# Other queue orders for the delta stage of a two-layer block on one Trainium2 core

## Chip, cores and metric

The kernel runs on one core of one Trainium2 chip. The metric is the device time of one execution in microseconds (us), lower is better. Times of several executions are given as their median.

## What is computed

Two transformer blocks, one after the other, over 256 positions of width 1024: the first has a gated feed-forward, an mLSTM mixer and a second feed-forward; the second has a gated delta rule layer, a feed-forward with a short convolution, a sliding-window attention and a last feed-forward. All in float32. Only the gated delta rule layer matters for this change:

```python
def gated_deltanet(hn, w_in, conv_w, a_log, dt_bias, out_norm_w, w_out):
    proj = hn @ w_in
    qkv, z, b, a = jnp.split(proj, [...], axis=-1)
    qkv = jax.nn.silu(causal_dwconv(qkv, conv_w))          # four taps
    q, k = l2norm(q) * 128 ** -0.5, l2norm(k)              # 8 heads, repeated to 16
    beta = jax.nn.sigmoid(b)
    g = -jnp.exp(a_log) * jax.nn.softplus(a + dt_bias)
    o = chunked_gated_delta_rule(q, k, v, g, beta)         # triangular solve, then hops
    o = rmsnorm_2(o, out_norm_w) * jax.nn.silu(z)          # 16 heads of 128
    return o.reshape(bsz, t, GDN_V_DIM) @ w_out
```

The solve inverts, for each head and chunk, a unit lower triangular matrix made of the products of the keys with a decay.

## The kernel before

Everything is a sequence of matrix products with weights streamed from HBM. A **unit** is 8 weight tiles of 128 x 128 (512 KB). For each unit SyncE (SP) loads it into one of four `raw` slots, ScalarE (ACT) makes its high part (`hi(j)`, `split_hi`, line 408), VectorE (DVE) or GpSimd (POOL) its low part (`lo(j)`, `split_lo`, line 417), and TensorE (PE) multiplies each tile three times (high x high, high x low, low x high) with 256 columns. A load waits for the low part of the unit four before it, a high part for PE's end of the unit four before it.

The delta stage is the class `GCore` (lines 1933 to 3314). It runs 52 units (`self.units`, numbered from 4 on PE), cut into **quarters** of two tiles, six matmuls: `d(h0, h1)` (line 3008) runs quarters h0 to h1 - 1, and quarter h is of unit h // 4. Between them stand the small products of the layer. The result banks rotate: `self.banks` gives the bank of unit j, `evicted` says which step empties it. The steps, by name:

- `sc`, `tap3_j`, `taps(j)`: scale, and the four taps of the convolution of unit j's result (ACT does tap 3, DVE taps 2 to 0). `zc`, `zx`, `zs`: the same for the gate z. `gzs(u)` scales the group u of z that was computed before the stage.
- `ggd1`, `ggd2`, `ggb` on DVE, `ea`, `gabs`, `exp_`, `ln_g`, `eb`, `gcs` on ACT: the decay g (its cumulative sum) and beta; `ggb` is an addition and the reciprocal of beta. `colsT` on PE transposes both and waits for both.
- `xs`, `xh`, `xl`: the normalised input in high and low part, for the units from 12 on. `qs`, `sq`, `ss`, `ln2`, `ln3`, `ex`, `kn`: Silu and L2 norm of q and k.
- `gk`, `mt`: products of keys, masked; `gather(g)`, `wld`: their diagonal blocks, through HBM, to one block per partition; `b(j)`: 31 steps of forward substitution on DVE in tile `gX`; `xt` (ACT): its transpose.
- `xd`, `xtd` (SP): stores of both to `x_d` and `xt_d`; `scatU` (4 DMAs, waits for `uzero`, a memset of POOL, which waits for `at(3)`) and `scatT` (3 DMAs) scatter the blocks back from there. Both wait for both stores. `gq`, `at`, `qd`: products of q and k, masked, and q with its decay.
- `c1` to `c8`, for four groups of heads: the rest of the solve, from 32-wide to 128-wide blocks, alternating PE (odd) with DVE (`c2`, `c6`) and ACT (`c4`, `c8`). `c1(0)` waits for all scatters.
- `p1` to `p7`, `e1` to `e6`, `kd`: the two chunks of the recurrence by group. `sqr`, `p7`, `rl`, `re`, `yz`, `yo`, `yh`, `yl`: norm, gate, and the high and low part of the result, which units 44 to 55 (`gout0`, `gout1`) multiply; unit 44 + 2u waits for `yl(u)`.

The order of each engine's queue is written out by hand in the methods `act`, `dve`, `pool`, `sync` and `pe`; the lists of names in `__init__` must repeat it, since a wait on a step is a wait on one counter per engine that has reached the place of that step in the list. Each engine executes its queue strictly in order, so a step that waits holds all behind it. `exp_and_log` (line 343) loads the ACT table that has Exp and Ln; where a Silu follows, another load comes by itself.

Of the kernel before, what the change touches and what calls it, by code (L numbers as in the profile page):

```python
# [154 lines left out]
def program(nc, a):  # L155
    with ExitStack() as ctx:
# [1637 lines left out]
        class GGateSteps:  # L1794
# [3 lines left out]
            def __init__(self, norm):  # L1798
                self.norm = norm
                self.dv = steps("dve", "ggate", ["a", "b", "pos", "b1", "beta", "gc0", "gc1"])  # L1800
                self.ac = steps("act", "ggate", ["abs", "eb", "exp", "ea", "ne", "ln", "gcs"])
# [131 lines left out]
        class GCore:  # L1933
# [5 lines left out]
            def __init__(self, gate, norm):  # L1939
                self.gate, self.norm = gate, norm  # L1940
                self.A = steps("act", "gdn_act", (
# [7 lines left out]
                    " yh3").split())  # L1949
                self.V = steps("dve", "gdn_dve", (  # L1950
# [13 lines left out]
                    " tap43_0 yl0 e1_3 e4_2 kd3 yz1 yo1 e1b_3 yz2 yl1 e4_3 yo2 yz3 yl2 yo3 yl3").split())  # L1964
                self.T = steps("pe", "gdn_pe", (
# [3 lines left out]
                    " p1k_3 p7_1 p5_2 p2_3 p6_2 p3_3 p1b_3 p7_2 p3b_3 p4_3 p5_3 p6_3 p7_3").split())  # L1969
                self.G = steps("pool", "gdn_pool", (  # L1970
                    "xzero col em0 em2 em3 xinit em1 br uzero tzero nb").split())
# [53 lines left out]
            def act(self, eng):  # L2025
# [186 lines left out]
                tap3(2)  # L2212
                tap3(0)
                tap3(1)
                hi(6)
                hi(7)
                exp_and_log(eng)
                tap3(3)
                gabs()
                eb()  # L2220
                exp_()
                ea()
                hi(8)
                tap3(4)
                ln_g()
                qs(0)
                gcs()
                tap3(5)
                hi(9)
                cols()  # L2230
                rp()
                tap3(6)
                hi(10)
                tap3(7)
                hi(11)
# [172 lines left out]
            def dve(self, eng):  # L2408
# [251 lines left out]
                for j in range(0, 4):  # L2660
                    b(j)
# [1531 lines left out]
```

How the kernel before makes its waits and increments, by code:

```python
    def wait(self, eng, it, name, back=0):  # L110
        n = len(self.names)
        eng.wait_ge(self.sem, (it + (1 - back)) * n + self.names.index(name) + 1)
# [216 lines left out]
        def unit_done(eng, st, it, u):  # L329
            eng.wait_ge(s_pe[u % SLOTS], turn(st, it, u) + 2)
# [7 lines left out]
        def evacuated(eng, st, it, g):  # L339
            eng.wait_ge(s_ev, group(st, it, g) + 5)
# [9 lines left out]
        def load_opening(eng, st, u):  # L351
            s = u % SLOTS
            eng.wait_ge(s_lo[s], turn(st, 0, u) + 1)
            eng.dma_start(raw[s][:, :, :].rearrange("p (g k) m -> p g k m", g=4),
                          st.weights[0].rearrange("p (g k) m -> p g k m", g=4)[:, :, 2 * u:2 * u + 2, :]
                          ).then_inc(s_raw[s], 16)
# [1 line left out]
        def load_keys(eng, u):  # L359
            eng.wait_ge(s_lo[u], turn(gqk0, 0, u) + 1)
            for b, s_body in enumerate((s_raw, s_kq)):
                eng.dma_start(raw[u][:, :, :].rearrange("p (g k) m -> p g (k m)", g=4)[:, 2 * b:2 * b + 2],
                              gqk0.weights[b].rearrange("p (g k) m -> p g (k m)", g=4)[:, 0:4:2, 2 * u * P:2 * (u + 1) * P]
                              ).then_inc(s_body[u], 16)
# [1 line left out]
        def load_pairs(eng, st, u):  # L367
            s = u % SLOTS
            eng.wait_ge(s_lo[s], turn(st, 0, u) + 1)
            eng.dma_start(raw[s][:, :, :].rearrange("p (g k) m -> p g (k m)", g=2),
                          st.weights[u % 2].rearrange("p (g k) m -> p g (k m)", g=2)[:, :, 4 * (u // 2) * P:
```

## Time and profile before

| | us |
|---|---|
| median of 3 runs | 1268.59 |
| lowest and highest | 1266.85, 1273.55 |
| profiled execution, its own time | 1265.16 |
| its span, first to last instruction | 1263.3 |
| PE / PE weight loads busy | 1238.2 (98%) / 1212.2 (96%) |
| DVE busy | 886.0 (70%) |
| ACT busy | 760.0 (60%) |
| POOL busy | 287.0 (23%) |
| mean granted TensorE clock | 0.995 |

The profiled execution is one run, 3.4 us under the median of the three. The delta stage runs from about 560 to 771 us of the span. PE's busy time is that of overlapping matmuls with modelled ends, so short stops don't show in it; the starts of the matmuls in the timeline do. Names of tiles in the rows are the program's: `gX`, `gXT` the substitution and its transpose, `gU`, `gT` the blocks, `dQK` q and k, `dVT` v, `wh`, `wl` the parts of the weights, `dZ` the gate, `H` the residual, `ACC` a sum of squares.

### The profile page before, as it was taken

Reading aid. Unit: us, or ns where it says so; the run is one execution under the profiler, and the core shown is the slowest. Engines: PE = TensorE matmul, PEld = TensorE weight load, DVE = VectorE, ACT = ScalarE, POOL = GpSimd, SP = SyncE. Lnnn points to the kernel's source line nnn. Section 1 sums busy time; section 2 is a strip of 40 time slices with the busy share of each in tenths; the row PEclk is TensorE's granted clock in tenths of the full one; section 3 lists DMA queues with packets and bytes.
Section 4 is the critical chain, followed back from the end, with each engine's and each line's share of the span. In section 5 each row is a group of like instructions: output and inputs, shape, how many; then the busy total and the mean of one; then the engine's idle time right before and its main releaser. Section 6 shows DMA issues by size and latency. Waiting matters only on the chain.

```text
span 1263.3 us, 28600 instructions
## 1 busy us (share of the span) xinstructions
PE 1238.2 (98%) x10498; PEld 1212.2 (96%) x10498; DVE 886.0 (70%) x1619; ACT 760.0 (60%) x1276; POOL 287.0 (23%) x243
## 2 busy tenths in 40 slices
PE   7999999999999999999999999999999999999997
PEld 7999999998999999999998989999999989999997
DVE  5866656887787665596777556777766797877654
ACT  6544444598555444469755686666665576766642
POOL 0000000010000000028875223344530131444400
PEclk9999999999999999999999999999999999999998
DMA  7655466464356656745646224855587525666473
GB/s 234 208 173 170 138 175 184 139 198 132 103 175 204 184 155 182 217 131 207 201 157 175 84 68 148 228 189 184 170 199 205 176 68 167 184 185 185 137 204 104
DMA packets 87804, 212.53 MB, mean 168 GB/s; under 512 B 19429, under 2 KB 34085, under 8 KB 87600
## 3 DMA queue, kind: packets, MB, share of 16 engines
q1 hardware_dynamic: 85536, 204.60, 53.7%
q0 software_dynamic: 1632, 6.46, 2.1%
q8 instruction: 49, 0.80, 0.3%
q10 hardware_dynamic: 560, 0.44, 0.1%
q14 instruction: 27, 0.22, 0.0%
HBM read 208.41 MB, written 3.06 MB: 167 GB/s over the span
## 4 chain that ended last, share of the span: by engine, by line
PE 89%; DVE 5%; ACT 3%; issue 2%; DMA 0%; POOL 0%; DVEq 0%; ACTq 0%; SPq 0%
PE bank L552 20%; PE bank L554 20%; PE bank L553 20%; PE bank L3002 3%; PE bank L3003 3%; PE bank L3004 3%; PE bank L525 1%; PE bank L1653 1%; PE bank L526 1%; PE bank L529 1%; PE bank L3137 1%; PE bank L1655 1%; PE bank L1654 1%; DVE wl L420 1%; PE bank L3654 1%
## 5 line engine op out<-in xcount | busy, mean ns | idle before, releaser
L415 ACT ACTIVATE wh<-raw 128x1024 fp32r<-128x1024 f32 (+3 forms) x423 | 407.4, 970 | 338.1 <-PE bank L554 286.4
L420 DVE TENSOR_TENSOR wl<-raw,wh 128x1024 fp32r<-128x1024 f32 (+3 forms) x350 | 384.6, 1102 | 138.7 <-ACT wh L415 138.1
L552 PE MATMUL bank<-XH,wh 128*128 128x256 f32 (+1 forms) x1448 | 410.7, 284 | 1.3 <-DVE XL L992 1.2
L554 PE MATMUL bank<-XH,wl 128*128 128x256 f32 (+1 forms) x1448 | 410.2, 283 | 0.0
L553 PE MATMUL bank<-XL,wh 128*128 128x256 f32 (+1 forms) x1448 | 409.9, 283 | 0.0
L552 PEld LDWEIGHTS bank<-XH,wh 128*128 128x128 f32 x1448 | 273.4, 189 | 2.1 <-DVE XL L992 1.4
L554 PEld LDWEIGHTS bank<-XH,wl 128*128 128x128 f32 x1448 | 273.7, 189 | 0.0
L553 PEld LDWEIGHTS bank<-XL,wh 128*128 128x128 f32 x1448 | 272.2, 188 | 0.0
L420 POOL TENSOR_TENSOR wl<-raw,wh 128x1024 fp32r<-128x1024 f32 x73 | 175.9, 2420 | 285.6 <-ACT wh L415 285.5
L552 PE MATMUL bank<-AH,wh 128*128 128x256 f32 (+1 forms) x704 | 198.7, 282 | 0.0
L554 PE MATMUL bank<-AH,wl 128*128 128x256 f32 (+1 forms) x704 | 198.5, 282 | 0.0
L553 PE MATMUL bank<-AL,wh 128*128 128x256 f32 (+1 forms) x704 | 198.2, 281 | 0.0
L553 PEld LDWEIGHTS bank<-AL,wh 128*128 128x128 f32 x704 | 132.8, 189 | 0.0
L554 PEld LDWEIGHTS bank<-AH,wl 128*128 128x128 f32 x704 | 132.3, 188 | 0.0
L552 PEld LDWEIGHTS bank<-AH,wh 128*128 128x128 f32 x704 | 132.1, 188 | 0.2
L3002 PE MATMUL bank<-gXH,wh 128*128 128x256 f32 x256 | 76.1, 297 | 1.8 <-DVE dVT L2452 1.8
L3003 PE MATMUL bank<-gXL,wh 128*128 128x256 f32 x256 | 72.2, 282 | 0.0
L3004 PE MATMUL bank<-gXH,wl 128*128 128x256 f32 x256 | 72.1, 282 | 0.0
L864 DVE TENSOR_TENSOR tp<-bank,R 128x256 f32<-128x256 f32 x88 | 37.3, 424 | 40.7 <-PE bank L554 33.2
L828 POOL TENSOR_TENSOR AL<-pr,AH 128x256 f32 (+1 forms) x44 | 36.6, 831 | 99.0 <-ACT AH L821 98.9
L3002 PEld LDWEIGHTS bank<-gXH,wh 128*128 128x128 f32 x256 | 48.9, 191 | 3.7 <-issue 3.2
L876 ACT ACTIVATE bank<-tp,vec 128x256 f32<-128x256 f32 x88 | 48.8, 554 | 4.5 <-DVE tp L864 4.5
(396 smaller groups left out, 2253.8 us busy)
## 6 DMA issues: line engine op xcount, KB each, us to landing
raw<-in_w_up SPq DMA_DIRECT2D x175, 512.0 KB, 4.4
raw<-in_w_down SPq DMA_DIRECT2D x64, 384.0 KB, 3.4
raw<-in_w_down SPq DMA_DIRECT2D x64, 320.0 KB, 3.2
raw<-in_w_gvz SPq DMA_DIRECT2D x32, 512.0 KB, 4.4
raw<-in_w_gout SPq DMA_DIRECT2D x16, 512.0 KB, 4.6
raw<-in_w_gqk SPq DMA_DIRECT2D x12, 512.0 KB, 4.6
raw<-in_w_mv SPq DMA_DIRECT2D x8, 512.0 KB, 4.6
raw<-in_w_mqk SPq DMA_DIRECT2D x8, 512.0 KB, 5.0
```

Source lines behind the costliest of these rows:

```text
L415: eng.activation(WH[s][:, 0:n, :], raw[s][:, 0:n, :], ACT.Copy).then_inc(s_hi[s], 1)
L420: eng.tensor_tensor(WL[s][:, 0:n, :], raw[s][:, 0:n, :], WH[s][:, 0:n, :].bitcast(F32), ALU.subtract).then_inc(s_lo[s], 1)
L525: eng.matmul(out, WH[u][:, 2 * g + j, :], xh, start=k == 0, stop=False)
L552: eng.matmul(out, WH[s][:, i, :], xh, start=start, stop=False)
L553: eng.matmul(out, WH[s][:, i, :], xl, start=False, stop=False)
L554: mm = eng.matmul(out, WL[s][:, i, :], xh, start=False, stop=stop)
L828: self.lows.done(eng.tensor_tensor(AL[:, bass.ds(j, 1), 0:T], PR[b][:, 0:T].unsqueeze(1), AH[:, bass.ds(j, 1), 0:T].bitcast(F32), ALU.subt ...
L864: leave(st, it, u, eng.tensor_tensor(TP[u % 2][:, 3:3 + T], bank[st.banks[u]][:, 0:T], R[:, 0:T], ALU.mult))
L876: self.tap2s.done(eng.activation(self.sums(u), TP[u % 2][:, 3:3 + T], ACT.Identity, bias=v(self.bias, m), scale=v(self.w, m + 88)), f"tap2 ...
L3002: eng.matmul(out, WH[s][:, i, :], xh, start=first, stop=False)
L3003: eng.matmul(out, WH[s][:, i, :], xl, start=False, stop=False)
L3004: mm = eng.matmul(out, WL[s][:, i, :], xh, start=False, stop=last)
```

## The change

The queues of the delta stage get another order on every engine, and the lists of names with them. No arithmetic is added or left out. One low part moves between engines in the sum: on DVE 13, 38, 43, 49, 50 become 14, 37, 50, 54; the others are POOL's. There are seven `exp_and_log` in both, at other places. The core of the diff:

```diff
 # pe: quarters between the small products
-                d(102, 104)
+                d(105, 107)
                 gq(0)
-                d(104, 115)
+                d(107, 113)
                 gq(1)
-                d(115, 132)
+                d(113, 128)
                 gq(2)
-                d(132, 136)
+                d(128, 133)
                 gq(3)
-                d(136, 156)
+                d(133, 148)
                 p1(0)
-                d(156, 158)
+                d(148, 159)
                 c1(0)
-                d(158, 159)
-                c1(1)
+                d(159, 161)
                 c3(0)
...
                 p6(3)
-                d(188, 191)
+                d(188, 190)
                 p7(3)
-                d(191, 208)
+                d(190, 208)
 # sync
                 xd()
                 xtd()
                 load(40)
-                load(42)
-                scatT()
                 scatU()
-                for j in range(43, 45):
-                    load(j)
-                load(41)
+                scatT()
+                load(41)
+                load(43)
+                load(42)
+                load(46)
...
 # dve, opening
-                taps(2)
-                ggd1()
-                ggb()
-                sc(4)
-                taps(3)
-                gzs(3)
-                ggd2()
-                taps(4)
+                sc(2)
+                ggd1()
+                taps(2)
+                ggd2()
+                gzs(3)
+                sc(4)
+                taps(3)
+                taps(4)
+                ggb()
...
 # dve, solve
-                b(30)
-                at(2)
-                taps(30)
-                qd(2)
+                at(2)
+                b(28)
+                taps(30)
+                b(29)
+                qd(2)
+                b(30)
                 qd(3)
                 taps(31)
                 at(3)
                 taps(32)
-                lo(38)
                 taps(33)
+                lo(37)
...
 # dve, way out
                 yo(2)
+                lo(50)
                 yz(3)
                 yl(2)
                 yo(3)
-                lo(50)
                 yl(3)
+                lo(54)
 # act, around the transpose and in the solve
-                tap3(33)
+                hi(36)
                 xt()
                 tap3(34)
+                hi(37)
                 hi(38)
-                hi(39)
                 vs(0)
+                hi(39)
...
                 c4(0)
+                hi(42)
+                vs(1)
                 c4(1)
...
-                hi(54)
                 hi(55)
+                hi(54)
 # pool
-                lo(33)
                 lo(34)
+                lo(33)
                 lo(35)
-                lo(37)
+                br()
                 lo(36)
-                br()
+                nb()
                 uzero()
+                lo(38)
+                tzero()
                 lo(39)
                 lo(40)
-                tzero()
-                nb()
+                lo(42)
                 lo(41)
```

## Rows read from the trace of the kernel before

**Rows 1.** Page, busy us and shares; the chain that ended last, by engine.

```profile
PE 1238.2 (98%) x10498; PEld 1212.2 (96%) x10498; DVE 886.0 (70%) x1619; ACT 760.0 (60%) x1276; POOL 287.0 (23%) x243
...
PE 89%; DVE 5%; ACT 3%; issue 2%; DMA 0%; POOL 0%; DVEq 0%; ACTq 0%; SPq 0%
```

**Rows 2.** Waits of PE, 540 to 790: engine, line, releaser; us, times, longest.

```profile
PE bank L3002 <- DVE dVT L2452: 1.8, 1, 1.8
PE bank L3002 <- DVE dZ L1078: 1.0, 1, 1.0
PE bank L552 <- DVE H L986: 0.9, 1, 0.9
PE bank L3137 <- DVE gVB L2559: 0.5, 1, 0.5
```

**Rows 3.** Windows: stretch, its us, busy us (instructions) by engine, PEclk, DMA share, GB/s.

```profile
560.00:765.00 205.00, 201.26 (x1955) 191.73 (x1954) 139.24 (x283) 148.07 (x234) 114.50 (x59) 0.99 0.47 143
```

**Rows 4.** Timeline of PE: start, us, instruction, [idle before, releaser].

```profile
568.35 0.28 PE L3003 MATMUL bank<-XL,wh 128*128 128x256 f32 x1
568.47 0.28 PE L3004 MATMUL bank<-XH,wl 128*128 128x256 f32 x1
569.71 0.36 PE L3002 MATMUL bank<-XH,wh 128*128 128x256 f32 x1 [0.95 <-DVE dZ L1078]
...
666.79 0.28 PE L3004 MATMUL bank<-gXH,wl 128*128 128x256 f32 x1
668.90 0.36 PE L3002 MATMUL bank<-gXH,wh 128*128 128x256 f32 x1 [1.84 <-DVE dVT L2452]
...
671.37 0.41 PE L3002 MATMUL bank<-gXH,wh 128*128 128x256 f32 x1
671.58 0.41 PE L3003 MATMUL bank<-gXL,wh 128*128 128x256 f32 x1
...
683.85 0.18 PE L3098 MATMUL bank<-gT,gMT 32*32 32x32 f32 x1
```

**Rows 5.** Windows, 670 to 672 (columns as in rows 3).

```profile
670.00:672.00 2.00, 2.00 (x11) 2.00 (x10) 1.93 (x4) 0.76 (x1) 1.99 (x1) 0.50 0.93 295
```

**Rows 6.** Timeline of DVE, opening, solve and way out.

```profile
565.75 1.75 DVE L1833 RECIPROCAL dB<-bank 16x256 f32<-16x256 f32 x1
...
639.50 0.42 DVE L2507 TENSOR_TENSOR dQK<-dQK,gEG 128x256 f32<-128x256 f32 x1
...
664.69 2.64 DVE L2507 TENSOR_TENSOR dQK<-dQK,gEG 128x256 f32<-128x256 f32 x1
...
774.18 2.62 DVE L999 TENSOR_TENSOR ACC<-ACC,sqb 128x256 f32<-128x256 f32 x1
```

**Rows 7.** Timeline of POOL.

```profile
664.58 4.98 POOL L420 TENSOR_TENSOR wl<-raw,wh 128x1024 fp32r<-128x1024 f32 x2 [1.30 <-ACT wh L415]
...
670.01 3.52 POOL L2800 MEMSET gU<- 128x4096 f32 x1
...
764.37 12.15 POOL L420 TENSOR_TENSOR wl<-raw,wh 128x1024 fp32r<-128x1024 f32 x5 [11.60 <-ACT wh L415]
```

**Rows 8.** Timeline of SP, DMA issues.

```profile
669.85 3.02 SPq L2882 DMA_DIRECT2D raw<-in_w_gvz  x2
672.91 3.76 SPq L2925 DMA_DIRECT2D gT<-x_d  x3
676.78 2.92 SPq L2917 DMA_DIRECT2D gU<-xt_d  x4
```

**Rows 9.** DMA issues, 660 to 700: out<-in, count, KB, median us to landing.

```profile
gU<-xt_d SPq DMA_DIRECT2D x4, 128.0 KB, 3.9
```

**Rows 10.** Timeline of ACT.

```profile
667.42 2.03 ACT L2141 ACTIVATE gXT<-gX 128x1024 f32<-128x1024 f32 x1 [1.60 <-DVE dQK L2507]
...
674.66 1.28 ACT L2161 ACT_TABLE_LOAD   x1
...
755.36 1.06 ACT L2195 ACTIVATE gRO<-dVT 128x1024 f32<-128x1024 f32 x1
```

More of the change, by code:

```diff
@@ L2256, in act @@
+                hi(16)
+                eg(2)
+                hi(15)
+                exa(1)
+                tap3(13)
+                eg(3)
                 exa(0)
                 exa(2)
-                tap3(12)
-                hi(16)
+                hi(17)
                 exa(3)
+                hi(19)
+                tap3(15)
                 sse()
-                tap3(13)
-                hi(17)
+                hi(18)
+                tap3(14)
                 brc()
-                exa(1)
@@ L2297, in act @@
+                ln2(1)
+                ex(2)
+                zc(21)
+                hi(27)
+                ln3(0)
+                zc(24)
+                zc(22)
+                hi(28)
+                zc(25)
+                lnr()
+                hi(29)
                 ln3(1)
-                zc(22)
+                exp_and_log(eng)
                 zc(23)
                 ex(3)
-                zc(24)
-                zc(25)
+                hi(30)
+                zc(26)
                 exr()
-                hi(29)
@@ L2398, in act @@
                 re(3)
-                hi(50)
                 yh(3)
@@ L2658, in dve @@
                 taps(17)
-                wb()
-                for j in range(0, 4):
-                    b(j)
-                taps(18)
-                for j in range(4, 7):
-                    b(j)
-                taps(19)
-                for j in range(7, 16):
+                taps(18)
+                taps(19)
+                wb()
+                for j in range(0, 11):
                     b(j)
                 kn(2)
-                for j in range(16, 19):
+                for j in range(11, 18):
                     b(j)
                 qd(0)
-                for j in range(19, 22):
-                    b(j)
                 at(0)
-                b(22)
-                kn(3)
-                qd(1)
-                for j in range(23, 27):
+                for j in range(18, 21):
                     b(j)
                 at(1)
+                kn(3)
+                for j in range(21, 24):
+                    b(j)
+                qd(1)
+                b(24)
+                b(25)
                 taps(28)
+                b(26)
+                taps(29)
                 b(27)
+                at(2)
                 b(28)
-                taps(29)
+                taps(30)
                 b(29)
+                qd(2)
                 b(30)
-                at(2)
-                taps(30)
-                qd(2)
                 qd(3)
@@ L2698, in dve @@
                 taps(36)
+                e1(0)
                 taps(37)
@@ L2702, in dve @@
                 c2(1)
-                kd(0)
-                e1(0)
+                c6(0)
                 c2(2)
-                c6(0)
+                taps(39)
                 c6(1)
                 c2(3)
-                taps(39)
                 e1b(0)
+                kd(0)
                 taps(40)
@@ L2928, in sync @@
                     load(j)
-                load(8)
+                for j in range(8, 10):
+                    load(j)
                 load(11)
                 load(10)
-                load(9)
                 for j in range(12, 14):
@@ L2936, in sync @@
                 load(14)
-                for j in range(16, 20):
+                load(16)
+                load(18)
+                load(17)
+                load(19)
+                gather(1)
+                gather(2)
+                for j in range(20, 22):
                     load(j)
                 gather(0)
-                gather(2)
-                load(20)
+                bst()
                 gather(3)
-                bst()
-                load(21)
-                gather(1)
+                load(22)
                 bld()
                 wld()
-                for j in range(22, 29):
+                for j in range(23, 28):
                     load(j)
-                load(30)
                 load(29)
+                load(28)
+                for j in range(30, 32):
+                    load(j)
+                load(33)
                 load(32)
-                load(31)
-                for j in range(33, 36):
-                    load(j)
-                load(37)
+                load(34)
                 load(36)
-                for j in range(38, 40):
+                load(35)
+                for j in range(37, 40):
                     load(j)
@@ L2962, in sync @@
                 load(40)
+                scatU()
+                scatT()
+                load(41)
+                load(43)
                 load(42)
-                scatT()
-                scatU()
-                for j in range(43, 45):
+                load(46)
+                for j in range(44, 46):
                     load(j)
-                load(41)
-                for j in range(45, 48):
+                for j in range(47, 49):
                     load(j)
+                load(51)
+                load(50)
                 load(49)
-                load(48)
-                load(50)
-                load(51)
             def pe(self, eng):
```

354 lines of the change are left out of this document (169 added, 185 removed), and 44 rows, old and new, of the table WP.

## The prediction

> **What bounds the kernel now.** I read the page from the top. Busy shares come first [rows 1]: TensorE (PE) is at 98% of the span, every other engine at 70% or less, and the chain that ended last lies on PE for 89%. So an edit counts only where it takes away or adds time in which PE stands still. The waits of PE come next [rows 2]: the delta stage with its way out (about 560 to 785 us) owns 1.8, 1.0, 0.9 and 0.5 us of them, 4.2 us in all. The windows [rows 3] say the same: PE is busy for 201.26 of 205 us, and no other engine passes 148. That already caps the gain. The change adds and removes no matmul, so PE's own work stays. All that can be won here is 4.2 us of waits, the slow clock that one of them causes (below), and short stops that the modelled ends of the matmuls hide.
>
> A figure for all that follows: in a steady row of weight matmuls the starts are 0.12 us apart [rows 4] (0.118 over longer rows). A quarter of a unit is six of them, **0.71 us**; a unit is 2.83.
>
> **The largest stop.** At 666.79 PE issues the last matmul before unit 35 (quarter 140) and goes on at 668.90 [rows 4], released by the taps of unit 31, whose bank unit 35 needs. A normal start would have been at 666.91, so the stop costs 2.0 us. After it the matmuls start 0.21 us apart instead of 0.12 until about 672.4, (672.4 - 668.9) / 0.21 = 17 of them: 17 x 0.095 = 1.6 us. The granted clock from 670 to 672 is 0.50 [rows 5], so the engine ran at 1.2 GHz instead of 2.4 after the stop. The 0.95 us stop before 569.71 [rows 4] was not followed by that. Together the place costs **3.6 us**.
>
> Why were the taps late? The second half of `qd(3)` took 2.64 us [rows 6] where the same instruction takes 0.42 at 639.50, when GpSimd (POOL) was idle. At 664.58 POOL had begun two low splits, 4.98 us together [rows 7], so some 2.4 each, and the DVE instruction ended when that one did. So DVE lost 2.2 us to POOL. The Trainium skill, "SBUF — State Buffer", Who interferes with whom, says that a DVE instruction with two SBUF inputs waits for a GpSimd instruction that reads SBUF, and not for one that only writes; the trace agrees (2.64 against 0.42).
>
> **The change, part by part.** The engines' queues of the delta stage are permuted; each engine keeps its arithmetic except one low split.
>
> *1. Quarters 133 to 140.* `gq(3)`, which releases `qd(3)`, moves from before quarter 136 to before quarter 133. Between it and unit 35 there are now 7 quarters, 4.95 us, where there were 4, 2.83 us. DVE must first do what follows `gq(2)`: `at(2)` 1.2, `b28` to `b30` 1.5, `taps(30)` 1.4, `qd(2)` 0.7, together 4.8 us; `gq(3)` ends five quarters and a gram after `gq(2)`, 4.4 us, so DVE is some 0.5 us late for it. Then come `qd(3)` (0.7) and `taps(31)` (1.43): 2.7 to 2.9 us behind `gq(3)`, of 4.95. With one POOL split in the way (2.2 more) it is 5.0, a tie. I take the stop as gone: **-3.6 us**. Bounds: -3.6 if it fits, 0 if DVE arrives as late as now.
>
> *2. Opening.* `gzs(3)` now stands behind `ggd2` instead of behind `ggb`, `sc(4)` and `taps(3)`. DVE reaches it at about 566.5, so PE doesn't stop at 568.47 [rows 4] (1.1 us back). But `ggb`, which held DVE for some 2.1 us (an addition of 0.4 and the reciprocal of 1.75 [rows 6]), now stands behind `taps(4)`: 563.2 + 1.2 (`ggd1`) + 1.4 + 0.65 (`ggd2`) + 0.35 + 0.35 + 2 x 1.43 = 570.05, and 2.1 more is 572.2. The column transposes of PE wait for it after quarter 27, which PE now reaches at 571.4. Added wait 0.75 us; behind it on PE stand quarters 28 on, and no other engine. Net **-0.4** (bounds -1.1 and +0.3, if the reciprocal comes as late as the stop now lasts).
>
> *3. Scatters.* Now SP stores `xt_d` just after the transpose `xt` (667.42 [rows 10], 2.0 us) and then sits in two weight loads, 40 and 42, until 672.87 [rows 8], since load 42 waits for `lo(38)`; only then come the three `scatT` and four `scatU`, to 679.70 [rows 8]. The last, issued about 0.7 us before that, lands some 3.9 us later [rows 9], at about 683, and `c1(0)` starts at 683.85 [rows 4]: little or no slack now. After the change load 42 stands behind the scatters, and `scatU` is first, so it waits for POOL's `uzero` (3.52 us [rows 7]), which follows `lo(36)` and `at(3)`. `xt` can start at about 665.6 (the step before it on ACT is then `hi(36)`, and the taps' order no longer holds it), `uzero` ends at about 671.6 (`lo(36)` from 665.6 takes 2.4, then 3.5), and with the same 10 to 10.5 us from first issue (672.91) to last landing the scatters land at about 682.1: about 1 us earlier. PE reaches `c1(0)`, now behind quarter 158 and not 157, at 683.6 - 3.6 - 0.4 + 0.7 = 680.3, with `gq` and `p1(0)` ahead of it in both; I add 0.5 us for near ties on the way (`lo(33)` now stands on POOL behind `lo(34)`, whose high part waits for unit 30, so that two splits of 2.4 us end within about 0.1 us of quarter 132; `vs(0)`, whose table load alone takes 1.28 us [rows 10], ends within 0.3 us of `p1(0)`). That leaves a new wait at `c1(0)` of **+1.3 us** and the near ties' **+0.5**. Bounds of both: 0 and 3.5 (scatters as late as now, about 683.3, and 0.5). What queues behind the wait: the whole solve on PE; ACT and DVE then have nothing urgent.
> The Trainium skill, "DMA: Bandwidth & Descriptors", Specifications, gives 512 B as the least transfer for full rate. The scatters are 128 B pieces: 7 x 128 KB [rows 9] in 10.4 us is 88 GB/s, against 295 GB/s in the stretch 670 to 672 [rows 5], so the trace agrees that their rate is low, and turning the two kinds round doesn't change it.
>
> *4. Solve and hops (quarters 159 to 190).* The orders are looser: `c3(0)` gets two quarters of cover after `c1(0)` where `c1(1)` had one, `e1(0)` moves far forward. The wait of 0.5 us for VB [rows 2] and some shorter ones have cover: **-0.5** (bounds -0.7, 0). Against this `p7(3)` moves from three quarters behind `p6(3)` to two: 1.42 us of cover, while its operand is ready 1.94 us after `p6(3)` (0.25 latency, then an eviction of 0.6 and the square until 756.42 on ACT [rows 10]). **+0.5** (bounds 0, +0.6). `hi(42)` now stands in front of `vs(1)` and `c4(1)`, and load 42 is issued behind scatters and load 43: see the slower rival.
>
> *5. Engines' loads.* Low splits on DVE go from 13, 38, 43, 49, 50 to 14, 37, 50, 54: one fewer (1.22 us), one more on POOL (2.4). ACT gets two more table loads (13 instead of 11, counting those that Silu after Exp and the reverse force), 2 x 1.28 us [rows 10], beside 40% idle time [rows 1]: nothing, where cover stands.
>
> *6. Way out.* PE stops for a residual sum H on DVE, 0.9 us by the wait [rows 2], 1.1 us with the restart. Its chain holds an ACC sum of 2.62 us at 774.18 [rows 6] while POOL splits until 776.5 [rows 7]; free of POOL, it should be nearer to the 0.42 of a product of that size. `lo(54)` leaves POOL, which then ends 2.4 us earlier. But `lo(54)` on DVE waits for `hi(54)`, now behind `hi(55)`, which waits for unit 51 (about 770.5); behind it on DVE stand the residual sums that now run at 767.92. The two largely cancel: **-0.4** (bounds -1.1, +1.5).
>
> **Sum** against the profiled execution: -3.6 - 0.4 + 1.3 + 0.5 - 0.5 + 0.5 - 0.4 = -2.6 us, say -3 (hidden short stops of the solve go with the looser order). The span was 1263.3 us, with 1.9 around it 1265.2; the median of the three runs is 1268.6 (1266.9 to 1273.6). The difference applied to the median gives 1266; I put it at **1265.5**.
>
> **Rivals.** *Same total, other stop (B).* The stop before unit 35 stays in part: `qd(2)` and `qd(3)` both meet a POOL split (2 x 2.2 us, with `lo(35)` then `lo(36)` just there), the taps come 2 us late, the clock falls again. Then step 1 gives 0, and the scatters, no longer overtaken, cost nothing: -0.5, about 1268. For it: POOL is busy for 4.98 us on end there [rows 7]; against it: three quarters more of cover.
>
> *Slower (C).* Load 42. It is issued behind seven scatters and load 43, at about 680, and needs 5 to 6 us in a full DMA (share 0.93 [rows 5]). ACT stands at `hi(42)` with `vs(1)` and `c4(1)` queued behind it, PE at `c5(1)`. By my count load 42 may land up to 6.3 us after `c1(0)` starts; I expect 4. From 6.3 us on each us is a us of PE. If the scatters land 3 us later than now (they share the DMA with load 40) and load 42 4 us beyond its slack, two stops over 1.8 us each bring the half clock (1.6 each): 3 + 4 + 3.2 - 3.6 - 0.4 + 1 = +7, about 1276. Against it: all these rows leave 2 us.
>
> *Faster by more (D).* Every stop goes and no new one comes: -3.6 - 1.1 - 0.7 - 1.1 = -6.5, about 1262. Against it: the 1.2 us of step 3 and the reciprocal of step 2.
>
> *The change doesn't do what it says (E)*: stores and scatters aren't nearer in time, since `scatU` waits for `uzero`; PE then gains only by `gq(3)`. It is within the forecast.
>
> **How the numbers follow.** The forecast (with E) 0.57, around 1265.5; B 0.20, 1268; C 0.09, 1276; D 0.14, 1262. A difference of under 0.5% (6.3 us) is about what a measurement of this kernel can't tell from none. The bounds of the unknown costs add to about -6 and +3 beside the forecast; with D and half of the runs' spread of 6.7 us the range is 1260.5 to 1271.5, C left out. Faster by over 0.5% (under 1262.3) is half of D and the low edge of the forecast: 0.15; slower (over 1274.9): 0.09; within: 0.76.
>
> **What would show it.** Of the changed kernel: no gap of 1.8 us and no clock under 1 near quarter 140 (step 1); a gap of 0.7 us before the column transposes instead of the one three units in (step 2); a wait for DMA before the first 32-wide matmul, `c1(0)`, about 1 us (step 3); a gap of 0.5 us before the last norm sums `p7(3)` (step 4); the wait for H on the way out unchanged or gone (step 6). A PE sum of waits in 560 to 785 over 4.2 us, or a second stretch at clock 0.5, would make the forecast wrong.

## The result, and the profile after

| | before | after |
|---|---|---|
| executions beside each other | 17 | 17 |
| median, us | 1267.68 | 1264.84 |
| lowest and highest | 1265.81, 1275.31 | 1263.25, 1271.26 |
| executions at 1270 us or more | 7 | 1 |
| mean | 1269.88 | 1265.29 |
| profiled execution, its own time | 1265.16 | 1264.78 |
| its span | 1263.3 | 1263.0 |
| mean granted clock of it | 0.995 | 0.998 |

The ratio of after to before is **0.9966, 95% interval 0.995 to 0.9981**: so the change makes the kernel some 0.2 to 0.4% faster, less than the 0.5% that counted as a difference. The medians are 2.8 us apart (0.22%), the means 4.6 (0.36%); the ratio lies nearer to that of the means, since the few long executions weigh in it. The two profiled executions are only 0.4 us apart, so their spans alone would have said "nothing happened".

The times of the kernel before fall into two groups with a gap between. Over all series here (110 executions) 70 took 1265.1 to 1268.6 us and 40 took 1270.8 to 1277.5, with a mean clock of 0.987 to 0.994 in the long ones against 0.995 to 0.999 in the others (in the 93 for which it is on record). In the series of the table the lower group has its median at 1266.9, in the four others at 1266.1 to 1266.6. So the change has two effects: in like executions it gains 2.1 us (1266.9 to 1264.8; 1.3 to 1.8 if the lower group of another series is taken), and it makes the long executions rare (7 of 17 before, 1 of 17 after). Both had to be explained.

The waits of PE between 540 and 790 us of the profile after (engine, line, releaser; us in total, times, longest), to be held against [rows 2]:

```profile
PE bank L552 <- DVE H L986: 1.8, 1, 1.8
PE bank L1887 <- DVE dB L1833: 0.7, 1, 0.7
PE bank L3205 <- ACT gRO L2195: 0.4, 1, 0.4
PE bank L3134 <- issue: 0.3, 1, 0.3
PE bank L3101 <- DVE dVT L2452: 0.2, 1, 0.2
```

The 1.8 us for `dVT`, the 1.0 for `dZ` and the 0.5 for `gVB` are gone; 0.7 us at the column transposes, 0.4 at `p7(3)`, 0.2 at `c1(0)` are new, and the wait for H has doubled. The sum is 3.4 us where it was 4.2. The window of the delta stage, with the columns of [rows 3]:

```profile
560.00:765.00 205.00, 203.44 (x1981) 194.06 (x1980) 138.39 (x281) 151.91 (x237) 123.11 (x62) 1.00 0.47 146
```

PE is busy for 2.2 us more of the same 205 us than in [rows 3], issues 26 matmuls more in it (x1981 against x1955), and the mean granted clock of the stretch is 1.00, where it was 0.99 before, with the stretch of [rows 5] at 0.50. The timeline of PE after, at the places of [rows 4] and of the forecast:

```profile
573.10 0.20 PE L1887 MATMUL bank<-cst,dA 16*128 16x16 f32 x1 [0.70 <-DVE dB L1833]
...
681.34 0.18 PE L3101 MATMUL bank<-gT,gMT 32*32 32x32 f32 x1 [0.17 <-DVE dVT L2452]
...
753.68 1.98 PE L3205 MATMUL bank<-gRO,ones 128*128 128x512 f32 x4 [0.36 <-ACT gRO L2195]
...
781.54 0.36 PE L552 MATMUL bank<-YH,wh 128*128 128x256 f32 x1 [1.85 <-DVE H L986]
```

These are column transposes, `c1(0)`, `p7(3)`, and the restart on the way out. Before, `c1(0)` stood at 683.85 [rows 4]; the timeline of before has the others at

```profile
756.66 1.88 PE L3202 MATMUL bank<-gRO,ones 128*128 128x512 f32 x4
...
782.89 0.36 PE L552 MATMUL bank<-YH,wh 128*128 128x256 f32 x1 [0.94 <-DVE H L986]
```

A ledger can be made from these starts. The stage began 0.8 us later in the execution of after (561.0 against 560.2), and quarters are worth 0.71 us each:

| stretch | before | after | quarters moved | net of them |
|---|---|---|---|---|
| entry to `c1(0)` | 123.65 | 120.34 | +1 | -4.0 |
| `c1(0)` to `p7(3)` | 72.81 | 72.34 | -2 | +0.95 |
| `p7(3)` to the restart | 26.23 | 27.86 | +1 | +0.9 |
| entry to the restart | 222.7 | 220.5 | 0 | -2.2 |

So the stage gives 4.0 us before the solve and gives 1.85 us of it back behind. The net -2.2 is near the 2.1 us between like executions of this series. The profiled spans hide it: after the entry offset, a 1.2 us wait in the attention of the second block (`L3693 <- DVE sSB L3507`) that this execution has takes up the rest. The same wait stands in the profiles of two of the variants of after below and is missing in four others, so it isn't a price of the change's own.

### The profile page after: what moved, and what is told of

The parts are those of the page before. It is cut to its first block, busy times and chain, and to the rows that moved or that the text cites. A ratio compares the mean times of both kernels' runs of the same rounds, so it can differ in the third digit from the quotient of the medians.

```text
span 1263.0 us, 28602 instructions
## 1 busy us (share of the span) xinstructions
PE 1236.8 (98%) x10498; PEld 1210.8 (96%) x10498; DVE 886.2 (70%) x1618; ACT 762.7 (60%) x1278; POOL 290.1 (23%) x244
## 4 chain that ended last, share of the span: by engine, by line
PE 90%; DVE 5%; ACT 3%; issue 2%; DMA 0%; POOL 0%; DVEq 0%; ACTq 0%; SPq 0%
PE bank L552 20%; PE bank L554 20%; PE bank L553 20%; PE bank L3005 3%; PE bank L3006 3%; PE bank L3007 3%; PE bank L1653 1%; PE bank L3140 1%; DVE wl L420 1%; PE bank L1655 1%; PE bank L1654 1%; PE bank L525 1%; PE bank L529 1%; PE bank L526 1%; PE bank L3658 1%
```

## The experiments

Names beginning with b are edits of the kernel before, with a of the changed one; each was timed beside the kernel before in the same series. The changed kernel itself was timed only in the series of the table, so a distance between it and a variant is one between series. In the text "lower group" is the executions of the kernel before under 1270 us of that series.

### What was the stop before unit 35?

**b_gq** gives the kernel before the changed places of `gq(2)` and `gq(3)` and nothing else:

```diff
-                d(115, 132)
+                d(115, 128)
                 gq(2)
-                d(132, 136)
+                d(128, 133)
                 gq(3)
-                d(136, 156)
+                d(133, 156)
```

> The kernel before with one edit on PE: gq(2) stands before quarter 128 and gq(3) before quarter 133, as in the changed kernel; every other queue as before. Theory A (unit 35 stopped because gq(3) came only four quarters ahead of it): the stop before unit 35 and the slow clock after it are gone, 3.6 us less than the kernel before, ratio 0.997. Rival P (the lost time is DVE held by a POOL split, and the order on PE alone doesn't move that): qd(2) or qd(3) meets a split as before, the taps of unit 31 are late again, at most 1 us less.

Measured 1271.79 us (1269.4 to 1275.37, 6 executions) against 1266.82: ratio 1.003, 1.0005 to 1.0056. **b_port** instead keeps PE's order and gives one low split of POOL to DVE, so that POOL is idle when `qd(3)` runs:

```diff
                 taps(32)
+                lo(37)
                 lo(38)
...
                 lo(35)
-                lo(37)
                 lo(36)
```

> The kernel before with one edit: lo(37) moves from POOL to DVE, behind taps(32). POOL then stands idle until hi(36) is done, about 665.5, so no split runs beside qd(3) at 664.35. PE's order is that of before (gq(3) before quarter 136). Port theory (the 2.64 us of qd(3) are a wait for the POOL split): qd(3) takes 0.42 twice, the taps of unit 31 end at about 666.5, no stop, no slow clock: 3.6 us less, ratio 0.997. Rival A (only gq(3)'s place counts), or qd(3) slow for another reason (the store of gX that starts at 663.69): the stop stays, 0 us.

Measured 1271.81 us (1266.07 to 1273.63), ratio 1.0018, 0.9991 to 1.0045. DVE in b_port, first, and its waits of PE:

```profile
664.20 0.42 DVE L2507 TENSOR_TENSOR dQK<-dQK,gEG 128x256 f32<-128x256 f32 x1
...
665.37 0.42 DVE L2507 TENSOR_TENSOR dQK<-dQK,gEG 128x256 f32<-128x256 f32 x1
```

```profile
PE bank L3098 <- DMA gU<-xt_d: 2.3, 1, 2.3
...
PE bank L3002 <- DVE dVT L2452: 0.3, 1, 0.3
```

Both edits remove the stop (in b_port the 2.64 us of the product of [rows 6] become 0.42, and the wait for `dVT` is 0.3). b_gq is slower for it; b_port has the same median, but its interval holds 1, so that by itself it isn't shown to be slower (four of its six executions are above 1270 us, four of the eleven of the kernel before beside it). In b_gq, whose stage began 1.5 us later than that of before, `qd(3)` meets no split either, since POOL's next two come later:

```profile
665.46 0.41 DVE L2506 TENSOR_TENSOR dQK<-dQK,gEG 128x256 f32<-128x256 f32 x1
665.80 0.41 DVE L2507 TENSOR_TENSOR dQK<-dQK,gEG 128x256 f32<-128x256 f32 x1
```

```profile
667.12 4.79 POOL L420 TENSOR_TENSOR wl<-raw,wh 128x1024 fp32r<-128x1024 f32 x2 [2.20 <-ACT wh L415]
```

That is 105.5 us behind the entry of the stage, where these splits began at 104.4 before. The taps of unit 31 end at 106.0 behind the entry, and PE is due for unit 35 at 106.8. With a split over `qd(3)` they would end some 2.2 us later and PE would stop for about 1.4 us (an estimate from these rows). So b_gq doesn't show that the earlier `gq(3)` removes the stop by itself.

In both PE now reaches `c1(0)` some 2 us before the last scatter has landed, and a stop of 2.0 to 2.3 us comes there. What follows it is the costly part. Windows of b_gq (columns as in [rows 3]):

```profile
684.00:688.00 4.00, 3.10 (x118) 2.86 (x118) 1.26 (x3) 0.00 (x0) 0.00 (x0) 0.82 0.98 280
688.00:700.00 12.00, 12.00 (x235) 11.35 (x229) 4.94 (x11) 5.37 (x12) 2.35 (x1) 0.50 0.25 88
700.00:708.00 8.00, 8.00 (x49) 7.66 (x48) 1.49 (x4) 3.66 (x5) 0.00 (x0) 0.56 0.01 2
708.00:712.00 4.00, 4.00 (x83) 3.63 (x82) 2.62 (x5) 1.18 (x3) 0.00 (x0) 1.00 0.00 0
```

The clock is 0.50 (1.2 GHz) for some 20 us. Before, the stretch from `c1(0)` to `p7(3)` took 72.8 us at clock 1.00; in b_gq and b_port it takes 81.2 and 81.3. So in these profiled executions a stop of some 2 us brought 1.6 us more in the row of weight matmuls, and 8.4 more at the head of the solve. Removing the stop alone only moves it to the dearer place.

**a_gq** asks the converse, the changed kernel with `gq(3)` back before quarter 136:

```diff
-                d(128, 133)
+                d(128, 136)
                 gq(3)
-                d(133, 148)
+                d(136, 148)
```

> The changed kernel with gq(3) back before quarter 136 (four quarters ahead of unit 35), nothing else. Theory A: the stop before unit 35 comes back with the slow clock, 3.6 us more than the changed kernel, as slow as the kernel before. Port theory: in the changed kernel POOL's next split starts only at 666.08, behind hi(36), so qd(3) at about 664.3 meets none, the taps of unit 31 end at 666.4 against 666.8 for unit 35: 0 to 0.3 us more.

Measured 1263.61 us (1262.76 to 1265.3), ratio 0.9964, 0.994 to 0.9987: the same as the changed kernel. There is no stop, and in this order too `qd(3)` gets in ahead of POOL's next split (0.43 us at 664.84 and 0.42 at 665.18, the split at 665.38, so closely). So in the changed kernel the stop goes by when POOL splits; the place of `gq(3)` adds margin to that, no time. **a_port** puts the collision back into the changed kernel: ACT makes `hi(36)` before `tap3(33)`, so POOL's `lo(36)` begins some 2 us earlier.

```diff
-                tap3(33)
                 hi(36)
+                tap3(33)
```

> The changed kernel with ACT's hi(36) in front of tap3(33), so that GpSimd's split lo(36) begins some 2 us earlier, about 663.5 us, and lies over qd(3) of VectorE at 664.2. Theory (a VectorE product with two operands in SBUF waits for a GpSimd split that runs at the same moment, which made the stop before unit 35 of the kernel before): qd(3) takes 2 to 2.7 us instead of 0.42, the taps of 31 end some 2 us later, TensorE stops 1 to 2 us about 666 to 669 us, and the time is 1 to 3.6 us above that of the changed kernel, 1266 to 1268.5. Rival (the stop came of where gq(3) stood on TensorE): qd(3) may be slow but no stop comes, and the time is 1264.5 to 1265.

Measured 1265.44 us (1264.65 to 1268.16), ratio 0.9976, 0.9956 to 0.9995. POOL, DVE and PE in a_port, whose stage began 0.5 us earlier in the execution:

```profile
663.49 2.40 POOL L420 TENSOR_TENSOR wl<-raw,wh 128x1024 fp32r<-128x1024 f32 x1
```

```profile
663.69 2.48 DVE L2506 TENSOR_TENSOR dQK<-dQK,gEG 128x256 f32<-128x256 f32 x1
```

```profile
668.10 0.36 PE L3005 MATMUL bank<-gXH,wh 128*128 128x256 f32 x1 [1.26 <-DVE dVT L2452]
```

and the same places in the changed kernel:

```profile
664.19 0.42 DVE L2506 TENSOR_TENSOR dQK<-dQK,gEG 128x256 f32<-128x256 f32 x1
```

```profile
666.08 2.43 POOL L420 TENSOR_TENSOR wl<-raw,wh 128x1024 fp32r<-128x1024 f32 x1 [2.06 <-ACT wh L415]
```

The mechanism is as expected: the product ends 0.3 us behind the split (663.69 + 2.48 = 666.17, 663.49 + 2.40 = 665.89), and PE stops for 1.26 us before unit 35. In the same series the changed kernel less its 0.7 us wait (a_ggb, below) has 1263.72, so the stop costs about 1.0 us in the median (an estimate, as the 0.7 us isn't measured in the times); the price is at the bottom of what was expected, and in the profiled execution the clock stayed at 1.00 behind the stop. There `c1(0)` starts 122.0 us behind the entry, 1.7 us later than in the changed kernel's. Five of the twelve executions lie at 1266.0 to 1268.2.

### What do the scatters do?

**a_scat** puts load 42 back in front of the scatters in the changed kernel:

```diff
                 load(40)
+                load(42)
                 scatU()
                 scatT()
                 load(41)
                 load(43)
-                load(42)
```

> The changed kernel with load 42 back in front of the scatters on SP, nothing else. Load 42 waits for lo(38), which POOL now makes behind its memset of U and ends at about 674.5. If the nearness of stores and scatters matters, the first scatter is issued at about 674.9 instead of 672.23 and shares the DMA with load 42: the scatters land 3 to 4 us later, c1(0) waits 3 us with a slow clock after it, 4 to 5 us more than the changed kernel. Rival (c1(0) has slack, as its wait in the changed kernel is for taps and not for a DMA): at most 1 us more.

Measured 1281.48 us (1270.06 to 1283.59), ratio 1.008, 1.0042 to 1.0118. The waits of PE in its profiled execution, one of the two short ones (1270.06 us):

```profile
PE bank L3101 <- DMA gT<-x_d: 4.0, 1, 4.0
```

SP in a_scat, and in the changed kernel:

```profile
668.72 6.35 SPq L2880 DMA_DIRECT2D raw<-in_w_gvz  x2
675.17 4.20 SPq L2915 DMA_DIRECT2D gU<-xt_d  x4
679.41 3.46 SPq L2923 DMA_DIRECT2D gT<-x_d  x3
```

```profile
672.23 2.14 SPq L2915 DMA_DIRECT2D gU<-xt_d  x4
674.41 2.55 SPq L2923 DMA_DIRECT2D gT<-x_d  x3
```

Behind load 42 the seven scatters start 2.9 us later and take 7.7 us to issue instead of 4.7, and `c1(0)` starts at 685.61 instead of 681.34. That is 4.3 us of late start; the stretch from `c1(0)` to `p7(3)` takes 73.3 us instead of 72.3, and the time of that execution is 5.3 us longer. The other executions, four at 1281 to 1284 us with a mean clock of 0.982 to 0.985, are some 11 us longer still, at the lower clock; none of them was profiled, so where they lose it isn't seen.

**b_scat** does it the other way round, load 42 behind the scatters in the kernel before:

```diff
                 load(40)
-                load(42)
                 scatT()
                 scatU()
+                load(42)
```

> The kernel before with one edit on SP: load 42 stands behind the seven scatters instead of in front of them. In the kernel before c1(0) starts within 0.3 us of the landing of the last scatter; where it has to wait 2 us (kernels b_gq and b_port), the granted clock is 0.50 for some 20 us of the solve that follows. Theory S (the slower executions of the kernel before, 1271 to 1275 us at a mean clock of 0.990 to 0.994, 4 of 11, are those in which the scatters land late): the scatters land about 1.5 us earlier, the stop before unit 35 stays (3.6 us), the lower times stay at 1265 to 1267, and no execution is above 1270; the median falls by 0 to 1 us. Rival (the slower executions have another cause): 3 in 10 of the runs are still above 1270.

Measured 1265.74 us (1264.3 to 1269.45, 12 executions) against 1266.9, ratio 0.9979, 0.996 to 0.9999. None of the 12 is above 1270 us, where 14 of the 35 executions of the kernel before beside it are. Against the lower group (median 1266.3) the gain is only 0.5 us. So this edit's gain is nearly all in the missing long executions. The same holds for the changed order: of the 53 executions of a_gq, a_port, a_ggb, a_hi and best none is long (that of 2432 us left out), where a_scat, with load 42 in front, has all six at 1270 us or more. Its windows around the stop, and those of the kernel before:

```profile
668.00:672.00 4.00, 2.18 (x18) 2.21 (x19) 3.86 (x9) 3.34 (x3) 3.90 (x4) 1.00 0.54 216
672.00:676.00 4.00, 4.00 (x36) 4.00 (x35) 3.86 (x8) 2.99 (x3) 4.00 (x2) 1.00 1.00 247
```

```profile
668.00:672.00 4.00, 3.10 (x15) 3.13 (x16) 3.89 (x8) 2.76 (x3) 3.90 (x4) 0.65 0.60 205
672.00:676.00 4.00, 4.00 (x34) 4.00 (x34) 3.22 (x7) 2.39 (x3) 2.81 (x2) 0.92 0.89 266
```

The first pair is b_scat. It has the same 1.8 us stop, and the clock stays at 1.00 behind it; entry to `c1(0)` takes 122.5 us there and 123.7 before. So the slow clock after that stop, 1.6 us of my step 1, doesn't always follow it. Whether it was the execution or the moved load that kept the clock up isn't shown: of the kernel before two executions were profiled (before and b_again), and it fell in both.

**b_gqscat** makes the diffs of b_gq and of b_scat together:

> The kernel before with two edits: gq(2) and gq(3) before quarters 128 and 133 on PE (as in b_gq) and load 42 behind the scatters on SP (as in b_scat). b_gq alone was 4 to 5 us slower, since PE, with no stop before unit 35, came to c1(0) 2 us before the scatters landed. Theory S: with the scatters 1.5 us earlier the wait at c1(0) is under 0.7 us, the clock stays at 1.00 in the solve, and both gains show: 1263 to 1264 us, ratio 0.997, all of what the whole change gives. Rival (the wait at c1(0) stays over 1.5 us, as uzero or the transpose sets the scatters): 1269 to 1275 as b_gq.

Measured 1266.49 us (1263.54 to 1269.43), ratio 0.9971, 0.9949 to 0.9994: neither the 1263 to 1264 of the theory nor the 1269 and more of the rival. Five of 12 executions lie at 1263.5 to 1264.0, below the changed kernel's median; the seven others at 1265.9 to 1269.4, with mean clocks down to 0.992. The profiled one (1268.27 us) is of the second sort:

```profile
686.00:690.00 4.00, 3.30 (x162) 3.04 (x155) 2.05 (x4) 2.31 (x5) 0.94 (x1) 1.00 0.05 18
690.00:702.00 12.00, 12.00 (x87) 11.54 (x85) 3.12 (x7) 5.60 (x10) 1.41 (x1) 0.57 0.15 46
```

The stop before unit 35 and the wait for the DMA are both gone, and yet the clock falls at 690 us, after 0.7 us without work in the middle of the small matmuls (`L3099 <- issue: 0.7`). The stretch from `c1(0)` to `p7(3)` takes 78.2 us there. So load 42 behind the scatters takes away what b_gq lost, but both gains show in five of 12 executions only. Something else in the changed order must keep the clock in the solve.

**b_loose** tries what: b_gqscat, with quarters laid singly between the levels of the solve, near to the changed order.

```diff
                 d(158, 159)
                 c1(1)
+                d(159, 160)
                 c3(0)
-                d(159, 160)
                 c1(2)
+                d(160, 161)
                 c3(1)
                 c5(0)
+                d(161, 162)
                 c1(3)
                 c3(2)
+                d(162, 163)
                 c7(0)
                 c5(1)
+                d(163, 164)
                 p2(0)
-                d(160, 161)
                 c7(1)
-                d(161, 164)
                 p1b(0)
```

> The kernel before with gq(2) and gq(3) each eight units earlier, load 42 behind the scatters (both as in b_gqscat), and in the solve the first quarters laid singly between its levels, as the changed kernel has them, instead of all ahead of c1(0). Theory (the small matmuls of the solve stand too thickly one after the other in the old order, and that lets the clock fall to 0.50 there in more than half of the executions of b_gqscat): TensorE stays at 1.00 from 680 to 710 us, the median is 1263.0 to 1264.5 and at most 2 in 10 executions stand above 1266. Rival (what lets the clock fall is something else in this order, such as the way the core reaches c1(0)): the median stays at 1265.5 to 1267 and half of the executions or more stand above 1266.

Measured 1264.35 us (1263.5 to 1274.31, 13 executions), ratio 0.9963, 0.9943 to 0.9982. Twelve of the 13 lie at 1263.5 to 1265.0, with mean clocks of 0.996 to 0.999, where b_gqscat had seven of 12 above 1265.8. So by the times, though none of the twelve was profiled and the two series are not the same, the spread quarters keep the clock, and with three edits the kernel before has the time of the changed one. The expectation of clock 1.00 in the profile failed, because the profiled execution was the one at 1274.31. Its wait and its windows:

```profile
PE bank L3098 <- DMA gU<-xt_d: 0.7, 1, 0.7
```

```profile
684.00:686.00 2.00, 1.94 (x41) 1.69 (x39) 1.16 (x4) 0.00 (x0) 0.00 (x0) 0.81 0.92 322
686.00:708.00 22.00, 22.00 (x317) 20.34 (x317) 6.78 (x14) 8.82 (x17) 2.35 (x1) 0.50 0.10 32
```

Here the scatters landed 0.7 us after PE had come to `c1(0)`, and the whole head of the solve, 22 us, ran at 1.2 GHz; `c1(0)` to `p7(3)` took 83.4 us. That is a long execution seen from within, though not one of the kernel before itself. It also bounds what the spread quarters and the moved load do: here PE had to wait at `c1(0)` with both in place, and the clock fell.

**b_again** is the kernel before, unchanged, to catch one of its own:

> The kernel before itself once more, unchanged, to see what the executions at 1271 us and above are. Theory (in these no stop before unit 35 is followed by a slow clock; instead TensorE reaches c1(0) before the scatters have landed and the clock is 0.50 for about 20 us from 684 us): about 2 in 5 executions at 1271 to 1276 and the rest at 1265 to 1268.5; should the profiled one be of the longer kind, it shows a wait for gU or gT at c1(0) and a clock of 0.50 from about 684 to 706 us. Rival (they are slow in some other place): a profile of the longer kind shows its slow clock elsewhere.

Six of its 12 executions took 1270.8 to 1275.6 us at mean clocks of 0.988 to 0.994, and six 1265.7 to 1267.4 at 0.996 to 0.998. The profiled one was of the short sort (span 1263.9 us), with the 1.8 us stop and clock 0.50 from 670 to 672 us as in [rows 5]. So where the long executions of the kernel before lose their 7 us is inferred, not seen: b_gq, b_port and b_loose show a loss of that size (8.4 to 10.6 us) at the head of the solve with the same mean clocks (0.988 to 0.990), and with load 42 alone moved none of 12 executions is long. The expectation that a profile would show them is neither met nor refuted.

### What did the change give back?

**a_hi** puts `hi(54)` before `hi(55)` on ACT in the changed kernel:

```diff
                 hi(53)
-                hi(55)
                 hi(54)
+                hi(55)
```

> The changed kernel with hi(54) and hi(55) turned round on ACT, nothing else. In the changed kernel DVE stands idle 8.9 us for hi(54), which stands behind hi(55), which waits for its raw tile until 768.6; lo(54) then meets a POOL split (2.59 us), and the residual sums come at 773.6 instead of 767.9; PE stops 1.85 us (2.1 with the restart). Queue theory: hi(54) runs at 765, lo(54) ends by 769, the sums follow, the stop is gone or under 0.5 us: 1.5 to 2 us less than the changed kernel, about 1262.8. Rival (the residual chain is set by hi(55) or by POOL's last split anyway): 0.9 us stop as in the kernel before, 1 us less.

Measured 1262.05 us (1260.74 to 1264.73 but for one execution of 2432 us, far outside all others), ratio 0.9945, 0.9924 to 0.9965. The stop on the way out is gone altogether. DVE on the way out, in the changed kernel and in a_hi:

```profile
770.66 2.59 DVE L420 TENSOR_TENSOR wl<-raw,wh 128x1024 fp32r<-128x1024 f32 x1 [8.93 <-ACT wh L415]
773.25 0.28 DVE L966 MEMSET ACC<- 128x272 f32 x1
773.57 0.76 DVE L986 TENSOR_TENSOR H<-bank,H 128x256 f32<-128x256 f32 x2
```

```profile
766.48 3.06 DVE L420 TENSOR_TENSOR wl<-raw,wh 128x1024 fp32r<-128x1024 f32 x1 [5.02 <-ACT wh L415]
769.55 0.28 DVE L966 MEMSET ACC<- 128x272 f32 x1
769.87 0.76 DVE L986 TENSOR_TENSOR H<-bank,H 128x256 f32<-128x256 f32 x2
```

With the high part earlier, `lo(54)` on DVE begins 4.2 us earlier and the residual sums behind it 3.7 us earlier, enough to meet PE. **a_ggb** takes away the wait of the column transposes:

```diff
-                taps(4)
                 ggb()
+                taps(4)
```

> The changed kernel with the ggb operation of VectorE one place earlier, ahead of taps(4). Theory (the 0.7 us wait of the column transposes is the taps of 4 standing in front of ggb): the wait is gone, nothing later takes it up, and the time is 0.7 us below the changed kernel's, 1264.0 to 1264.3. Rival (the taps of 4 are needed as early themselves): a stop of 0.5 us or more stands at the quarter that reads them, and the time is 1264.8.

Measured 1263.72 us (1262.22 to 1265.22), ratio 0.9964, 0.9944 to 0.9983. The wait is gone, the transposes stand at 571.66 instead of 573.10 (the stage began earlier in this execution), and no other takes it up. The 1.1 us against the changed kernel's 1264.84 is between two series; by the ratios (0.9964 and 0.9966) it can't be told from nothing. In its profiled execution the clock fell behind the 1.9 us stop on the way out, 0.50 from 782 to 784 us; in the changed kernel's it didn't.

**best** joins the two diffs and gives `p7(3)` its third quarter of cover back:

```diff
-                d(188, 190)
+                d(188, 191)
                 p7(3)
-                d(190, 208)
+                d(191, 208)
```

> The changed kernel with three edits: hi(54) and hi(55) turned round (as a_hi), ggb in front of taps(4) on DVE instead of behind it, and p7(3) behind three quarters instead of two on PE. Each aims at one stop of the changed kernel: 2.1 us on the way out, 0.70 before the column transposes, 0.36 before p7(3). If the stops add: 3 us less than the changed kernel, about 1261.5. Rival: the stops move (taps(4) 2.1 us later delays the high parts of the input, so that PE stops before quarter 48): 1.5 to 2 us less.

Measured 1261.24 us (1260.36 to 1266.83, 12 executions), ratio **0.995, 0.993 to 0.997**: 5.7 us under the kernel before in its series (5.0 under its lower group), as expected, and with a_hi the quickest of all. Between 540 and 790 us one wait of PE is left:

```profile
PE bank L3048 <- ACT gRT L2112: 0.5, 1, 0.5
```

## Why the prediction was right, step by step

The time (1265.5 forecast, 1264.84 measured), the sum of -2.6 us (stage -2.2, like executions -2.1) and "within 0.5%" were right. That the sum fits is partly luck. Up to `c1(0)` I had -2.2 us (steps 1 to 3), and it was -4.0; behind it I had -0.4 (steps 4 and 6), and it was +1.85: errors of 1.8 and 2.25 us that cancel. The time fits for one more such reason: of the 2.8 us between the medians 2.1 are between like executions, and the rest is the rarer long ones, for which the sum has no term.

**Step 1, -3.6, was right in the profile, and only half right in its cause.** Entry to `c1(0)` shortened by 4.0 us, which is -3.6 and the -0.4 of step 2. But I gave the gain to three more quarters of cover, and a_gq shows none for them in the changed order. What counts is that POOL pauses: DVE's `qd(2)` meets a split (2.18 us at 661.42), `qd(3)` none (0.42 at 664.19). I had this rule from [rows 6, 7] and used it only for the cause of the old stop. It should have been used for the new order too: when does POOL's next split start, and what releases it. Also 1.6 of the 3.6 us is a slow clock that doesn't always follow such a stop (b_scat).

**Step 2, -0.4, was right.** The wait at the transposes was forecast at 0.75 and is 0.70; the stop for `dZ` is gone; the transposes start at 573.10 - 561.0 = 12.1 us from entry, where they stood at 12.5 before.

**Step 3, +1.3 and +0.5, was wrong.** `c1(0)` waits 0.17 us, for the taps of unit 38, and not for a DMA. The mis-sized term is "the same 10 to 10.5 us from first issue to last landing". The scatters start at 672.23, as `uzero` allows (forecast 671.6), but their issue takes 4.7 us instead of 6.8 [rows 8], since no 512 KB load is in flight when they begin (the DMA share is 0.07 from 672 to 673); with the 3.9 us from issue to landing the last is down about 680.4 (an estimate), 8.2 us after the first issue. I had changed the loads' place and kept the duration that was measured with the load beside it. The near ties of 0.5 us were not seen in this stretch.

**Step 4, -0.5 and +0.5.** `p7(3)` waits 0.36 us, forecast 0.5. The wait for VB did go, but the stretch `c1(0)` to `p7(3)` didn't get shorter by it: net of quarters it is 0.95 us longer, of which 0.36 is `p7(3)`. The other 0.6 is partly in idle time at the 64-wide products of line 3134, two places and 0.8 us in all, for which the profile names no releaser; what causes it wasn't tried. So "a looser order gains" failed in the executions that I compared, by 1.1 us. Its worth seems to be one that I didn't price: it keeps the clock (b_gqscat against b_loose).

**Step 5, nothing**, stands: no wait names a table load.

**Step 6, -0.4, was wrong in sign:** +0.9. Its two halves were both named, and "the two largely cancel" was the failure. The sum of 2.62 us became 0.42 as said, but the residual sums moved from 767.92 to 773.57, 5.7 us, behind `lo(54)`. A shorter link on a chain whose head has moved by more can't help. Also `hi(55)` waited for its raw tile until 768.6 and not for PE's unit 51. The bound of +1.5 held it.

**What was not in the sum** is the gain from fewer long executions. I had the spread of three executions of the kernel before (1266.85 to 1273.55) and one row of slow clock [rows 5], and asked what that row cost here, not where else a stop of this length would cost more. By b_scat the long ones, 14 of 35 in its series, come of load 42 in front of the scatters. And the order of the two gains matters: had the change moved `gq` alone, my step 1 would have forecast -3.6, and the median of b_gq lies 5.0 us above that of before.

**The rivals.** B (the stop stays in part) is the a_port variant: it is real, at 1.0 to 1.7 us and not 3.6. C (load 42 late) didn't come: nothing in the solve waits for it, and its place behind the scatters is what gains. D (1262, all stops gone) was right as a picture of what was there to have: a_hi and best reach it, by undoing the two misplacements that my steps 2 and 6 had named.

## What to carry to other kernels

A stop of the bounding engine has a place as well as a length: before one is removed, follow the engine to its next meeting with a transfer, for it will arrive there earlier by what was gained, and the slow clock behind a stop of 2 us cost 8.4 us at the head of small dependent matmuls against 1.6 in a row of weight matmuls (in a_scat, behind 4.0 us at the same place, only about 1). Small scatters that something waits for go ahead of large loads in the queue, and their duration is to be taken without the load once it is moved. Where executions of a kernel fall into groups, compare like with like and ask for the cause of the groups by itself; a single profile of each kernel showed neither the gain of 2.1 us nor the groups.

## What the runs showed of the hardware that was not expected

- **The clock falls after some short stops and not after others.** After a stop of 1.8 to 1.9 us in rows of weight matmuls it fell to 0.50 in three profiled executions (before, b_again, and a_ggb on the way out) and stayed at 1.00 in four others (b_scat before unit 35; after, a_port and a_scat on the way out). What decides isn't known.
- **How long it stays low differs.** In the row of weight matmuls it was back after about 4 us (before, 668.9 to about 672.4). At the head of the solve, among 32- and 64-wide matmuls, it stayed at 0.50 for about 20 us (b_gq, b_port) and 22 us (b_loose). In a_scat a 4.0 us stop at the same place was followed by only about 4 us of it (between 684 and 690), so what follows the stop doesn't decide it alone. The Trainium skill, "TensorE: Matmul & The Clock Gate", A second HAM failure mode: psum-queue depth-cycling, says that frequent short idles between groups of matmuls can make the clock swing. In b_gqscat it fell at 690 us after one idle time of 0.7 us among small matmuls, which fits, though the cause of each fall wasn't isolated.
- **A busy DMA stretches the issue of small scatters.** The same seven issues, 128 KB each, took 4.7 us on SP in the changed kernel, with no large load in flight at their start, and 7.7 in a_scat, which differs only in load 42 just ahead of them. With load 42 ahead in the old order they took 6.5 to 6.8 (b_port, before) and 9.3 (b_gq); with load 40 alone, 5.2 (b_scat).
